# A fused two-block transformer kernel: the first window-attention gap of each delta-rule step placed behind the state matmuls, and one wait taken from GpSimd

## The reference

```
m = strict_lower((k*beta) @ k.T * decay); t_inv = inverse(eye + m)
u = t_inv @ (v*beta);  w = t_inv @ (k*beta*exp(g));  a = lower(q @ k.T * decay)
def step(state, ...):                      # one chunk after the other
    v_new = u - w @ state
    o     = (q*exp(g)) @ state + a @ v_new
    state = state*exp(g_last) + (k*exp(g_last-g)).T @ v_new
```

## Time and profile before

| | |
|---|---|
| median of 3 runs | 2409.59 us (2408.52, 2409.59, 2419.22) |
| profiled execution | 2408.52 us, span 2406.7 us |
| busy: PE, PEld, DVE, ACT, POOL | 2172.6, 1682.5, 1161.2, 730.5, 374.5 us |
| mean granted PE clock | 0.95 of full |
| the stage, 373.5 to 781: PE, DVE, ACT, POOL busy | 345.4, 246.8, 130.2, 111.5 of 407.5 us |

### The profile page before, as it was taken

One profiled execution on the slowest core, in us unless ns is written; L12 is line 12 of the kernel. 1 busy time (PEld: TensorE's weight loads), 2 busy tenths in 40 slices (PEclk: granted clock), 3 DMA queues, 4 the chain that ended last, 5 costly groups with the idle time before them and its releaser, 6 DMA issues. The chain is left out here.

```text
span 2406.7 us, 33809 instructions
## 1 busy us (share of the span) xinstructions
PE 2172.6 (90%) x14386; PEld 1682.5 (70%) x14414; DVE 1161.2 (48%) x1691; ACT 730.5 (30%) x1263; POOL 374.5 (16%) x305
## 2 busy tenths in 40 slices
PE   3999996888987899999948788899999999999998
PEld 2888884567766677777725354677878878878877
DVE  4575333666665764222167466546442443342443
ACT  3222313233332343111131466444221321221321
POOL 3000002222223651000032221252000000000000
PEclk9999997799898899999968899999999999999999
DMA  3212332000001745454200400322112112111112
GB/s 125 99 44 73 93 97 83 1 2 2 2 2 46 245 131 175 131 166 149 85 17 2 189 1 1 114 79 62 44 40 57 44 35 61 45 42 55 44 37 86
DMA packets 185209, 168.98 MB, mean 70 GB/s; under 512 B 13448, under 2 KB 163804, under 8 KB 184932
## 3 DMA queue, kind: packets, MB, share of 16 engines
q1 hardware_dynamic: 179006, 146.77, 19.5%
q0 software_dynamic: 5360, 19.92, 2.1%
q10 hardware_dynamic: 694, 0.13, 0.0%
HBM read 138.49 MB, written 28.31 MB: 69 GB/s over the span
## 5 line engine op out<-in xcount | busy, mean ns | idle before, releaser
L246 PE MATMUL mix_acc<-mix_hi,w_hi 128*128 128x512 f32 x1040 | 410.1, 394 | 8.6 <-DVE w_lo L234 8.6
L248 PE MATMUL mix_acc<-mix_hi,w_lo 128*128 128x512 f32 x1040 | 408.7, 393 | 0.0
L247 PE MATMUL mix_acc<-m_lo,w_hi 128*128 128x512 f32 x1040 | 408.6, 393 | 0.0
L229 ACT ACTIVATE w_hi<-w_stage 128x1024 fp32r<-128x1024 f32 x160 | 169.0, 1056 | 614.0 <-PE mix_acc L248 259.0
L234 DVE TENSOR_TENSOR w_lo<-w_stage,w_hi 128x1024 fp32r<-128x1024 f32 x160 | 199.6, 1248 | 229.3 <-ACT w_hi L229 229.3
L2750 DVE SCALAR_TENSOR_TENSOR hidden<-mix_acc,hidden_conv,hidden 128x1023 f32<-128x1023 f32 x88 | 112.9, 1282 | 263.5 <-ACT hidden L2709 261.9
L246 PEld LDWEIGHTS mix_acc<-mix_hi,w_hi 128*128 128x128 f32 x1040 | 195.3, 188 | 56.8 <-DVE w_lo L234 12.4
L248 PEld LDWEIGHTS mix_acc<-mix_hi,w_lo 128*128 128x128 f32 x1040 | 195.3, 188 | 45.1
L247 PEld LDWEIGHTS mix_acc<-m_lo,w_hi 128*128 128x128 f32 x1040 | 195.4, 188 | 44.3
L246 PE MATMUL acc<-h_hi,w_hi 128*128 128x512 f32 x432 | 170.8, 395 | 4.8 <-DVE h_lo L631 4.8
L247 PE MATMUL acc<-h_lo,w_hi 128*128 128x512 f32 x432 | 169.1, 391 | 0.0
(11 more groups left out here) (311 smaller groups left out, 3545.9 us busy)
## 6 DMA issues: line engine op xcount, KB each, us to landing
w_stage<-in_w_in SPq DMA_DIRECT2D x48, 512.0 KB, 5.4
w_ada<-in_w_ada SPq DMA_DIRECT2D x48, 512.0 KB, 4.8
w_stage<-in_w_up SPq DMA_DIRECT2D x44, 512.0 KB, 3.7
w_stage<-in_w_out SPq DMA_DIRECT2D x32, 512.0 KB, 4.1
spill<-y_tok POOLq DMA_DIRECT2D x24, 512.0 KB, 4.5
m_resid<-resid_spill SPq DMA_DIRECT2D x2, 4096.0 KB, 14.5
conv_in<-spill SPq DMA_DIRECT2D x3, 2048.0 KB, 12.3
w_stage<-in_w_down SPq DMA_DIRECT2D x16, 384.0 KB, 3.4
```

What stands on the lines that cost most here:

```text
L229: nc.scalar.activation(w_hi[:, slot], w_stage[:, slot], ACT.Copy).then_inc(w_hi_ready, 1)
L246: nc.tensor.matmul(acc[:, h, :], w_hi[:, slot, k, :], hi[:, k, tok], start=k == 0, stop=False)
L247: nc.tensor.matmul(acc[:, h, :], w_hi[:, slot, k, :], lo[:, k, tok], start=False, stop=False)
L248: mm = nc.tensor.matmul(acc[:, h, :], w_lo[:, slot, k, :], hi[:, k, tok], start=False, stop=k == kts - 1)
```

## The change

On PE, ACT and DVE the call of gap (0,0) moves from ahead of the state work to behind it. On POOL the wait for the end of `first_inverse(s)` ahead of `v_scaled(s)` goes.

```diff
@@ gpsimd
                     if s < NCH:
-                        pool.wait_ge(s_xu, STORED * s + 2)
                         v_scaled(s)
                         decayed(s)
@@ tensor (scalar and vector likewise)
                 for s in range(NCH + 1):
-                    in_gap(s, 0, 0)
                     if s:
                         state_sums(s - 1)
                     for lv in range(LEVELS):
@@
-                        if lv:
-                            in_gap(s, lv, 0)
+                        in_gap(s, lv, 0)
                         if s < NCH and lv:
                             inv_sum(s, lv)
```

## The result

The changed kernel took 2443.22 us (median of 6 runs, 2435.2 to 2445.8) against 2412.69 for the kernel before; the ratio is 1.0122, with a 95% interval of 1.0096 to 1.0148. One of the six runs of the kernel before took 5824 us and is left out of the ratio; without it that median is 2410.1. The change is slower, as forecast, but by more than twice the forecast: 30 to 33 us instead of 13.3, and outside the range. The profiled execution took 2445.64 us, 37.1 more than that of before.

What follows compares the result with a forecast made beforehand. The prediction took the PE-DVE chain, five times a step, to bound the stage, with no engine full. 9.4 + 1.6 + 1.4 + 2 = 14.4 us on the profiled 2408.52 gave 2422.9 us, within 2415 to 2430.

Steps and rivals of the forecast that it cites:

- GpSimd's products hold DVE up, 9.4 us net: Without the wait, products meet DVE's L1309 and L1315 in `first_inverse`: 11.5 us lost, part taken back, net 9.4 us slower.
- Odd steps, the two delays hide each other: Odd steps: ACT's later copy delays `turn1` 1.0 us, mostly hidden by GpSimd's delay; steps 3 and 15 make the sum 1.6.
- the third rival: GpSimd does not obstruct DVE where its products move; only the order costs, about 7 us: 2416 us, chance 0.12.
- Step 1, 2.3 us: In step 1 ACT's key squares wait behind `q_state_scale`, so `corner_sum` comes later: 2.3 us slower.
- Step 2, 0.9 us gained: In step 2 DVE no longer waits for `kb` but goes straight to L1343: 0.9 us gained.
- The second rival: `state_sums` fills PE's hole in step 2, so 441 to 475 runs at full clock: 2411 us, chance 0.13.
- PE's clock, 2 us between -8 and +9: More PE idle time in even steps 4 to 8 adds one short clock fall: 2 us, bounds -8 and +9.
- the other three terms: GpSimd's products 9.4 us, odd steps 1.6, and steps 1 and 2 together 1.4, all slower.
- the first rival: More idle PE in even steps brings another long fall of the clock, 8.3 us: 2431 us, chance 0.20.
- The price of a long fall, 8.3 us: The step with the half-clock stretch of 640 to 657 lasts 29.4 us against 21.1 for an ordinary even step: 8.3.
- the sign for a wrong forecast: L1309 and L1315 staying at 0.42 us in steps 4 to 9, or a clock over 441 to 475 far from 0.62.

Runs made afterwards that it cites:

- e5_fill_order: The moved gap alone, GpSimd keeping its wait, plus extra matmuls on PE, against the kernel before: 2407.52 us, ratio 0.9968.
- e1_order: The moved gap alone, GpSimd keeping its wait, no extra matmuls, against the kernel before: 2425.90 us, ratio 1.0057.
- e4_fill_before: The kernel before plus extra matmuls on PE where it stood idle, results overwritten, against the kernel before: 2390.65 us, ratio 0.9909.
- e8_fill_ends: The kernel before with extra matmuls in steps 1 to 15, and more around and in step 0 and in step 15: 2389.68 us, ratio 0.9897.

## Why the prediction was wrong, point by point

- *GpSimd's products hold DVE up, 9.4 us net:* right. L1309 and L1315 behaved as worked out in each step, and 10.4 us in the twelve steps with the same clock compare with the 8.4 that the forecast leaves without step 7. Single steps were off: step 4 cost 0.03 us, since L1394 fell back from 0.85 to 0.16 and DVE's idle time took up the rest, and steps 10, 12 and 14 cost 1.1, 0.4 and 1.1 instead of 0.63, 0 and 0.63, as the moved products met L1394 there (0.75 instead of 0.34 us). The prediction looked for that meeting in one place only.
- *Odd steps, the two delays hide each other:* right (0.96 in step 7 up to L1294, not 2). Steps 3, 9 and 11, which have no fall in either kernel, cost 0.95, 0.97 and 0.66 us. The order's bare prices without the products were 0.9 to 0.06, 2.0 in the five steps 5 to 13, below the 3.4 that the third rival was built on.
- *Step 1, 2.3 us:* the wait was right in kind (PE waited 1.85 and 0.87 us for ACT in `e5_fill_order`), and so was its bare price: in `e1_order` the step took 39.35 us against 38.10 and had 3 us less at the lower clock, 2.4 us together. In the changed kernel it brought a fall with it: 4.5 us.
- *Step 2, 0.9 us gained:* not to be seen in the time. The step took 38.60 us against 38.05, with 3.4 us more at the lower clock, which is 1.3 us by the price above; what is left is near the 0.9, but no run shows it by itself. The second rival, that the state matmuls would fill PE's hole and keep the clock up, fell: over 441 to 475 the clock was 0.66 against 0.62.
- *PE's clock, 2 us between -8 and +9:* this is the step that failed. The term measured 70 to 74 us more at the lower clock, at 0.39 us each 27 to 29 us. With the 12.4 us of the other three terms that makes 40 to 41, against 40.5 measured in the stage. The prediction had the mechanism, and the first rival named one more long fall; there were three (in steps 5, 12 and 13) and several short ones, while the one in step 10 got shorter.
- *The price of a long fall, 8.3 us:* misread. It was taken against 21.1 us for an ordinary even step, which is the length of an odd one; even steps without a fall took 22.8 and 22.9. The same step without its fall took 22.76, so the fall cost 6.6.

More could have been had from the rows. The prediction held against the first rival that most idle times of this size are followed by no fall. In the six even steps from 4 to 14, with 1 to 2 us of PE idle time from L1299 to the second turn, the trace of before had four falls (steps 6, 8, 10 and 14). The change put 1.2 to 2.4 us into every step from 3 to 14, where the odd ones had had 0.3 to 1.1, and the prediction still counted one fall more. Bounds of about one long fall either way were no bounds. Nor did the sign for a wrong forecast cover this: it watched the clock over 441 to 475, and the falls came elsewhere.

Why a fall at times lasts 3 us and at times 17 to 20, with PE as busy afterwards, is open; no run here tells it apart. Nor does the size of the idle time decide: in the kernel before, 2.0 us in step 4 had no fall behind them and 1.0 us in step 8 had one. The full price of the order in steps 2 and 15, where nearly every profile has falls, is open too. That GpSimd and DVE share something in SBUF is inferred from operand places and durations; no run changed the operands alone.

## What to carry to other kernels

A dependent chain of small matmuls can sit at the edge of PE's clock. Here delays of 12 us in sum cost 40. In such a chain each step that a delay gives more PE idle time has to be counted as a possible fall, not only as a wait. Before a wait is taken from an engine that nobody waits for, look at what runs beside it afterwards. Throw-away matmuls in PE's idle places are a cheap test of how much the clock costs, and here also a gain of 1%.

## What the runs showed of the hardware

- A GpSimd operation that reads SBUF and a DVE operation with two SBUF operands took turns: 1.07 or 1.08 us for the second DVE operation of `first_inverse`, which takes 0.42 undisturbed, in every one of steps 4 to 9 in each of the four kernels without the wait. The Trainium skill ("SBUF — State Buffer", Who interferes with whom) describes this as a lock on a shared port; the trace agrees, with 1.08 us for L1310 and an undisturbed 1.08 us for four L1338, which read one operand from PSUM, beside GpSimd's products.
- Extra work raised the speed: about 68 us less at the lower clock for 66 more matmuls, 22.5 us in time (`e4_fill_before`).
- Step 0 got no shorter by three extra matmuls a level: 21.67 us in `e8_fill_ends`, 21.63 in `e4_fill_before`. The clock rose in part of it (0.59 over the step instead of 0.50).
